# A hybrid decoder step on one core: one tile of a depthwise convolution moved to diagonal matrix products

## The chip, the cores and the metric

The kernel runs on one core of one Trainium2 chip. The metric is the device time of one execution in microseconds. Engines are named as in the profile: PE is the matrix engine (TensorE) and PEld its weight loads, DVE the vector engine, ACT the scalar engine, POOL is GpSimd, and SP issues most transfers. All arithmetic here is float32.

## The reference, cut to what matters

A single layer handles 512 prompt tokens and 8 sample tokens. A projection feeds two groups of channels.

```
z = x @ w_in
# group A: 512 channels
u = z[:, :512] * sigmoid(z[:, 512:1024])
c = causal_depthwise_conv(u, conv_w, width=31) + conv_b   # per channel: sum over k of w[k] * u[t - 30 + k]
c = silu(layer_norm(c))
# group B: 8 heads of 64, state S[value, key], for each token t
S_t = S_{t-1} diag(w_t) + (S_{t-1} a_t) b_t^T + v_t k_t^T ;  y_t = S_t r_t
o = (group_norm(y) + bonus) * gate
x = LN(ALPHA * x + concat(c, o) @ w_out)
x = LN(ALPHA * x + MoE(x))          # 64 experts, top 8, one shared expert
```

## The kernel before, in words

There are three stages. `prepare` projects, shifts and scales, solves small triangular systems and starts the convolution. `recur_and_mix` runs the recurrence, then the output projection, the norm, the router and the shared expert. `experts` streams the 64 experts' weights and multiplies.

**The convolution.** The channels lie on partitions in CT = 4 tiles of 128. `m.u_pad[:, i, :]` holds tile i with 30 zeros ahead of its 512 tokens. One tap (line 176) is one DVE instruction over 128x512: `conv[i] = u_pad[i, k:k+512] * w[:, k] + conv[i]`. There are 4 x 31 = 124 of them, and `Taps.take(n)` issues the next n in order. 74 are taken in `prepare`, fitted between its other DVE work, and 50 in the recurrence: 14 and 5 ahead of step 0, three in each of steps 0 to 9, one in step 10. The sum must be complete in step 10, as step 11 folds it for the norm's mean (line 1930), PE sums over partitions (`conv_sums`), step 13 subtracts it (line 2057), and ACT squares it in step 14.

**The recurrence.** 512 tokens are 16 steps (NCH) of L = 32 tokens. Four steps make a block j of 128 tokens (TM = 4 blocks). Here n is the step, j = n // 4 and c = n % 4. PE, ACT and DVE each run their own list in a fixed order written out by hand, with semaphores between them.

- PE, once a block: `push(j)` (line 1406, 64 products, one per head and chunk) writes `p_push`; ACT copies it to `pushed`; `solve(j)` (line 1415, 64 products with an output of 32x128) writes `p_solved`; ACT copies that to `w1` and `w2` (lines 1710, 1713).
- PE, twice a block: `moves_of(g)` (lines 1431, 1439, 1443) forms the transition and additive parts of two steps and of the reads. ACT copies them (lines 1720, 1721), and DVE adds a part into `r_dec` (`add_reads(g)`, line 1973). `moves_of(g)` waits for the copies and reads of g-1.
- PE, each step: `step(n)` (line 1455) multiplies the state by the step's transition, once the state of n is ready. DVE has meanwhile scaled the old state and added the step's part (lines 2025, 2027), does whatever else is listed for the step (taps, sample tokens' work, group norms), and last adds PE's product (line 2062), which releases `step(n + 1)`.
- PE, once a block: `outputs(j)` (lines 1469, 1475, 1478) reads the four states of the block, in step 4j+4. Its products per tile of two heads are 16 + 16 + 16.
- PE also has, among these, `late_column` (line 1583, the last two projected columns), `turn_tails` and `turn_out` (lines 1486, 1490, 1510), and `gates` (lines 1500, 1501).

In PE's list, step n is: `step(n)`; at n = 12 `conv_sums`; at n = 1 and 3 a late column; at c = 0 `outputs(j-1)` and then `push(j+1)`; at n = 0, 2, 4, 6, 8 a `turn_tails`; at c = 1 `solve(j+1)`; at n = 11 and 15 `gates`; at c = 2 and 3 a `moves_of`; at n = 14 `turn_out`. `outputs(3)` follows step 15, and then `conv_sums` and the output projection `mix_part` (line 1560, 128x512 products with 128x128 weights).

**Space.** The PSUM tensor `ph` has two halves of 1024 columns. `p_push` is the first 512 columns of the second half, `p_solved` all 1024 of it. `w_out` is loaded by SP (line 1284) into the space of the column weights `w_col`, after the last late column and the last solve.

Of the kernel before, what the change touches and what calls it, by code (L numbers as in the profile page):

```python
# [19 lines left out]
ALU = mybir.AluOpType  # L20
# [3 lines left out]
P = 128  # L24
D = 1024
KD = D // P
T = 512
# [4 lines left out]
DC = 512  # L32
# [972 lines left out]
def recur_and_mix(nc, m, ctx_out):  # L1005
# [14 lines left out]
    TAPS_OVER = 10  # L1020
    CONV = 11
    BIG = 1e30
    GONE = -3e38
    QD = D // 4
    with ExitStack() as ctx:
# [107 lines left out]
        sample_y_loaded = early_sem("sample_y_loaded")  # L1133
        tails_stored = [sem(f"tails_stored{b}") for b in range(2)]
        push_done = early_sem("push_done")
        push_taken = early_sem("push_taken")
# [113 lines left out]
        with nc.Block() as block:  # L1250
            @block.sync
            def _(sp):
# [106 lines left out]
            @block.gpsimd  # L1359
            def _(pool):  # L1360
                for spent in m.spent:
                    pool.sem_clear(spent)
                pool.sem_inc(spent_cleared)
                ch = Chain(pool, m.pool_step, m.pool_count)
                pool.wait_ge(w2_done, TM)
# [24 lines left out]

            @block.tensor
            def _(pe):
# [5 lines left out]
                def push(j):  # L1398

                    if j >= 1:  # L1400
                        pe.wait_ge(w1_taken, j)
                        pe.wait_ge(w2_taken, j)
                    for h in range(H):
# [4 lines left out]

                def solve(j):

                    pe.wait_ge(push_taken, j + 1)
                    for h in range(H):
                        for c in range(CM):
                            q, hc = slice(L * c, L * (c + 1)), slice(h * N, (h + 1) * N)
                            last = nc.tensor.matmul(p_solved[q, h, :, :], m.inverse[q, H * j + h, :], two(m.a_rows[q, j, hc], pushed[q, hc]),  # L1415
                                                    start=True, stop=True)
                    last.then_inc(w2_done, 1)

                def moves_of(g):
# [3 lines left out]
                    if g % 2 == 0:  # L1423
                        pe.wait_ge(w1_taken, j + 1)
                        pe.wait_ge(w2_taken, j + 1)
                    if g >= 1:
# [30 lines left out]

                def outputs(j):

# [3 lines left out]
                    if j >= 1:  # L1463
                        pe.wait_ge(centred, ORDER.index(j - 1) + 1)
                    for i in range(CT):
                        for h in (2 * i, 2 * i + 1):
# [4 lines left out]
                        for h in (2 * i, 2 * i + 1):  # L1471
# [7 lines left out]
                    last.then_inc(y_done, 1)  # L1479

# [105 lines left out]

                push(0)
                late_column(0)
                solve(0)
                late_column(1)  # L1590
                moves_of(0)
                moves_of(1)
                for n in range(NCH):
                    j, c = n // CM, n % CM
                    step(n)
                    if n == CONV + 1:
                        pe.wait_ge(conv_folded, 1)
                        pe.wait_ge(w1_taken, TM)
                        pe.wait_ge(w2_taken, TM)
# [12 lines left out]
                    if n in NORMALISE:  # L1612
# [5 lines left out]
                    if n in TURN:  # L1618
                        turn_out(ORDER[TURN[n]])
                outputs(TM - 1)  # L1620
                pe.wait_ge(conv_folded, 2)
# [74 lines left out]
            def _(act):  # L1696
# [3 lines left out]
                def copy_push(j):  # L1700
                    act.wait_ge(push_done, j + 1)
                    if j >= 1:
                        act.wait_ge(w2_done, j)
                    nc.scalar.copy(pushed[:], p_push).then_inc(push_taken, 1)

                def copy_solved(j):
                    act.wait_ge(w2_done, j + 1)
                    if j >= 1:
                        act.wait_ge(move_done, 2 * j)
                    nc.scalar.copy(w1.rearrange("p (h n) -> p h n", h=H), p_solved[:, :, 0, :]).then_inc(w1_taken, 1)  # L1710
                    if j >= 2:
                        act.wait_ge(y_done, j - 1)
                    nc.scalar.copy(w2[:, j % 2, :].rearrange("p (h n) -> p h n", h=H), p_solved[:, :, 1, :]).then_inc(w2_taken, 1)

# [63 lines left out]
                def take_column(u):  # L1778
# [4 lines left out]
                    if b == 1:  # L1783
# [3 lines left out]
                                         scale=m.keep[0:w, s:s + 1]).then_inc(row_taken, 1)  # L1787

                copy_push(0)
                take_column(0)  # L1790
                copy_solved(0)
                take_column(1)
                copy_moves(0)
                copy_moves(1)
                for n in range(NCH):
                    j, c = n // CM, n % CM
                    if n in ROOT:
                        root(ROOT[n])
# [13 lines left out]
                    if c == 1 and j + 1 < TM:  # L1812
                        copy_solved(j + 1)
                    if n in NORMALISE:
# [92 lines left out]
            def _(dve):  # L1907
# [106 lines left out]
                nc.vector.memset(stat[:], 0.0).then_inc(state_ready, 1)  # L2014
                taps.take(14)
                add_reads(0)
                taps.take(5)
                add_reads(1)
                for n in range(NCH):
# [7 lines left out]
                    ch.link(tt(new, new, moves[:, (n // 2) % SETS, n % 2, 1].rearrange("p (i n) -> p i n", i=CT), ALU.add))  # L2027
                    if c == 3 and j + 1 < TM:
                        add_reads(2 * j + 2)
                    if c == 0 and j >= 1:  # L2030
                        add_reads(2 * j + 1)
                    if n in INVERT:
# [15 lines left out]
                    if n == TAPS_OVER:  # L2048
                        taps.take(CT * CW - m.taps_done)
                        ch.link(tt(m.conv[:, :, T:TT], m.u_pad[:, :, CW - 1 + T:CW - 1 + TT], m.params[:, :, CW - 1:CW].broadcast_to([P, CT, B]), ALU.mult))  # L2050
# [8 lines left out]
                    if n in SUM:  # L2059
                        squares(SUM[n])  # L2060
                    dve.wait_ge(step_done, n + 1)
                    tt(new, new, pst[:], ALU.add).then_inc(state_ready, 1)
# [925 lines left out]
```

## Time and profile before

| what | us |
|---|---|
| median of 3 runs (lowest, highest) | 1083.47 (1079.4, 1086.22) |
| the profiled execution, its own time | 1083.88 |
| its span, first to last instruction | 1081.8 |
| PE busy in the span | 1026.4 |
| DVE busy | 710.3 |
| ACT busy | 228.2 |
| POOL busy | 327.6 |

A busy PE is not a PE at its peak: its products are pipelined, and its clock is granted at one of two levels, 2.4 GHz (1.00 in the profile) or 1.2 GHz (0.50). The share of an engine over the whole span says little here, since the stages have different limits. In the trace the recurrence's first product starts at 216.7 us, step 0 of DVE at 235.8, step 15 ends at 321.5, and the output projection starts at 329.8. All starts below are in us from the start of the span.

### The profile page before, as it was taken

The page shows a single profiled execution, that of the slowest core. Times are in us where ns is not written, and L with a number is a line of the kernel's source. Part 1 is how long each engine was busy: PE and PEld are TensorE (multiplying, and loading weights), DVE is VectorE, ACT ScalarE, POOL GpSimd, SP SyncE. Part 2 cuts the span into 40 slices and gives each one's busy share as a digit, 9 for nine tenths or more (in the row PEclk, how much of TensorE's full clock was granted, in tenths as well). Part 3 has the DMA queues.
Part 4 walks back from the last instruction along what each step waited for, and adds up shares of the span by engine and source line. Part 5 has one row for each costly group of instructions (what it writes and reads, how often), then busy time and mean ns, then how long its engine had stood idle before and what let it go on. Part 6 is the DMA issues. An engine that isn't in the chain of part 4 may idle for free.

```text
span 1081.8 us, 31303 instructions
## 1 busy us (share of the span) xinstructions
PE 1026.4 (95%) x13698; PEld 741.5 (69%) x13699; DVE 710.3 (66%) x1547; ACT 228.2 (21%) x480; POOL 327.6 (30%) x330
## 2 busy tenths in 40 slices
PE   8999999878889999999999999999999999999976
PEld 6877888665754458687767777777777777777742
DVE  0789869888876696975578555556555655565326
ACT  2145612122446312101111111011111111111114
POOL 2000010000000001445555455554455555555411
PEclk9999999878859999999999999999999999999997
DMA  7221222250066429599999999999999999999962
GB/s 227 78 60 39 59 60 84 43 163 3 7 205 241 171 83 373 194 356 382 389 390 389 378 384 390 385 386 387 388 385 395 392 387 387 389 389 376 353 197 107
DMA packets 92038, 282.64 MB, mean 261 GB/s; under 512 B 22552, under 2 KB 49689, under 8 KB 67061
## 3 DMA queue, kind: packets, MB, share of 16 engines
q1 hardware_dynamic: 74685, 243.55, 58.1%
q0 software_dynamic: 16272, 33.84, 12.2%
q10 hardware_dynamic: 944, 3.24, 0.8%
q8 instruction: 108, 1.77, 0.6%
q14 instruction: 29, 0.24, 0.1%
HBM read 260.93 MB, written 36.25 MB: 275 GB/s over the span
## 4 chain that ended last, share of the span: by engine, by line
PE 68%; DVE 8%; ACT 2%; DMA 1%; issue 1%; POOLq 0%; DVEq 0%; SPq 0%; ACTq 0%
PE ph L2378 32%; PE ph L2406 21%; PE ph L1542 3%; PE ph L1560 2%; DVE w_exp L176 1%; PE pz_late L1583 1%; PE ph L1683 1%; DMA scr_f<-arena,row 1%; PE pt L1475 1%; PE pz_late L1500 1%; PE pt L2539 1%; PE pz_late L1501 0%; PE pst L1455 0%; PE pt L1478 0%; PE pt L933 0%
## 5 line engine op out<-in xcount | busy, mean ns | idle before, releaser
L2378 PEld LDWEIGHTS ph<-arena,w_exp 128*64 128x64 f32 x8192 | 342.0, 139 | 51.3 <-issue 47.5
L2378 PE MATMUL ph<-arena,w_exp 128*64 128x96 f32 x8192 | 353.9, 248 | 2.1 <-DVE arena L2363 2.1
L2406 PE MATMUL ph<-w_exp,arena 128*96 128x512 f32 x512 | 235.1, 602 | 1.2 <-DVE arena L2396 1.2
L977 POOL DMA_INDIRECT x_area<-scr_x,piece_row x192 | 203.0, 1057 | 82.9 <-issue 54.7
L2433 POOL DMA_INDIRECT scr_f<-arena,row x63 | 93.9, 1490 | 215.1 <-PE ph L2378 166.7
L523 PE MATMUL pz<-w_exp 128*128 128x260 f32 x672 | 155.7, 389 | 0.3 <-ACT w_exp L335 0.3
L2406 PEld LDWEIGHTS ph<-w_exp,arena 128*96 128x96 f32 x512 | 78.4, 163 | 110.2 <-issue 102.1
L523 PEld LDWEIGHTS pz<-w_exp 128*128 128x128 f32 x672 | 128.0, 193 | 22.4 <-issue 2.7
L2424 DVE TENSOR_SCALAR arena<-ph,row_weight 96x512 f32<-96x512 f32 x64 | 47.8, 747 | 138.6 <-PE ph L2406 138.6
L2363 DVE STREAM_TRANSPOSE arena<-x_area 128x768 f32<-128x768 f32 x64 | 104.2, 1628 | 5.3 <-DMA x_area<-scr_x,piece_row 4.6
L2387 ACT ACTIVATE arena<-ph 128x192 f32<-128x192 f32 x64 | 21.1, 330 | 409.6 <-PE ph L2378 402.6
L176 DVE SCALAR_TENSOR_TENSOR w_exp<-arena,w_exp 128x512 f32<-128x512 f32 x120 | 90.0, 750 | 3.6
L2394 DVE TENSOR_TENSOR arena<-arena,ph 128x192 f32<-128x192 f32 x64 | 22.5, 351 | 89.5 <-ACT arena L2387 89.5
L2416 ACT ACTIVATE arena<-ph,row_weight 96x512 f32<-96x512 f32 x64 | 43.6, 682 | 111.6 <-PE ph L2406 101.1
L1560 PE MATMUL ph<-w_exp 128*128 128x512 f32 x128 | 56.9, 596 | 0.0
L955 DVE TENSOR_SCALAR piece_row<-found 32x3 uint32<-32x3 f32 x240 | 40.8, 170 | 4.4
L1560 PEld LDWEIGHTS ph<-w_exp 128*128 128x128 f32 x128 | 23.7, 190 | 28.8 <-issue 28.4
L809 POOL COPY w_exp<-w_exp 128x8 f32<-128x8 f32 x4 | 2.6, 653 | 125.3 <-DVE w_exp L727 125.3
L964 DVE COPY row_weight<-found 32x2 f32<-32x2 f32 x180 | 37.0, 205 | 3.1
L922 DVE TENSOR_TENSOR arena<-slot_index,position 128x480 bf16<-128x480 f32 x60 | 38.4, 645 | 0.0
L1374 POOL MEMSET arena<- 128x64 f32 x1 | 0.2, 151 | 110.0 <-PE ph L1572 110.0
L1366 POOL MEMSET arena<- 128x128 f32 x1 | 0.2, 204 | 106.6 <-PE ph L1415 106.6
(394 smaller groups left out, 1025.4 us busy)
## 6 DMA issues: line engine op xcount, KB each, us to landing
w_exp<-in_exp_up_dram SPq DMA_DIRECT2D x64, 1024.0 KB, 23.9
w_exp<-in_exp_down_dram SPq DMA_DIRECT2D x64, 1024.0 KB, 24.4
w_exp<-in_exp_gate_dram SPq DMA_DIRECT2D x64, 1024.0 KB, 21.8
w_exp<-in_w_in_dram SPq DMA_DIRECT2D x22, 512.0 KB, 3.7
w_exp<-in_x_prompt_dram SPq DMA_DIRECT2D x8, 512.0 KB, 5.4
w_exp<-in_w_out_dram SPq DMA_DIRECT2D x2, 2048.0 KB, 11.6
w_exp<-scr_f SPq DMA_DIRECT2D x8, 512.0 KB, 5.8
x_area<-scr_x,piece_row POOLq DMA_INDIRECT x192, 7.6
```

The source lines that it names most:

```text
L176: self.ch.link(self.nc.vector.scalar_tensor_tensor(out, u, w, out, ALU.mult, ALU.add))
L523: last = nc.tensor.matmul(banks(pz[0:w, c % 2, :])[:, b, :], m.w_col[:, c % WB, k, 0:w], halves(m.x_t[:, k, :])[:, b, :], start=(k == 0), ...
L922: nc.vector.tensor_tensor(m.members[:, e], m.slot_index[:].unsqueeze(1).broadcast_to([P, NT, CAP]), src.unsqueeze(2).broadcast_to([P, NT, ...
L955: last = nc.vector.tensor_scalar(m.piece_row[32 * quad:32 * (quad + 1), s, :], m.found[rows, :, 0], float(QUADS), float(QUADS * TT + quad) ...
L977: nc.gpsimd.indirect_dma_start(m.x_pieces[:, s, r, :], None, m.scr_x1.rearrange("t (q c) -> (t q) c", q=QUADS), bass.IndirectOffsetOnAxis( ...
L1560: last = nc.tensor.matmul(ph[0:n, i % 2, c * 512:(c + 1) * 512], lhs, w_out[c][:, kw, :], start=(part == 0 and k == 0), stop=(part == 1 an ...
L2363: nc.vector.transpose(x_list_t[:, s % 2].rearrange("p k (r t) -> p r k t", r=RUNS), m.x_pieces[:, s].rearrange("p r (c k) -> p r k c", k=K ...
L2378: last = nc.tensor.matmul(pgu[64 * half:64 * half + 64, s % 2, (2 * part + j) * CAP:(2 * part + j + 1) * CAP], w[job.slot][:, k, f0:P * ha ...
L2406: last = nc.tensor.matmul(pyl[0:CAP, c, :], hid[:, s % 2, j, :], m.expert_down[job.slot][:, j, c * 512:(c + 1) * 512], start=(j == 0), sto ...
L2416: nc.scalar.activation(y_list[:, s % 2, 0:512], pyl[0:CAP, 0, :], ACT.Copy, scale=row_weight[0:CAP, job.l, 1:2]).then_inc(y_act, 1)
L2424: nc.vector.tensor_scalar(y_list[:, s % 2, 512:1024], pyl[0:CAP, 1, :], row_weight[0:CAP, job.l, 1:2], None, ALU.mult).then_inc(y_dve, 1)
L2433: nc.gpsimd.indirect_dma_start(m.scr_f[s % 2], bass.IndirectOffsetOnAxis(ap=row[:, job.l:job.l + 1], axis=0), y_list[:, s % 2, :], None, b ...
```

## The change

Tile 3 of the convolution leaves the `Taps` list. For tap k ACT builds a diagonal 128x128 matrix, the identity scaled per partition by w[:, k], into one of 8 buffers, and PE multiplies it with `u_pad[:, 3, k:k+512]`, all 31 products accumulating in `p_conv`, a PSUM bank. In step 10 DVE copies that bank to `conv[3]` with the bias added. Of the 31 products, 2 stand behind `push(0)`, 4 between `moves_of(0)` and `moves_of(1)`, and 3, 2, 3, 2, 3, 3, 3, 3, 3 in steps 0 to 8. DVE keeps 93 taps: 74 in `prepare` as before, 9 ahead of step 0, and one in each of steps 0 to 9.

`p_solved` shrinks to 512 columns, and so `solve(j)` runs in two halves of four heads, each copied by ACT before the next overwrites it. `outputs(j)` is also in two halves, of tiles 0 and 1 in step 4j+4 and of tiles 2 and 3 in step 4j+5, with `push` ahead of the first. `add_reads` moves from the head to the end of its step's DVE list. The loads of `w_out` wait for the last diagonal too, since the diagonals lie in that space.

```diff
+    DIAGS = 8
+    LAST_TILE = CT - 1
+    CONV_TAPS = {0: 3, 1: 2, 2: 3, 3: 2, 4: 3, 5: 3, 6: 3, 7: 3, 8: 3}
...
-        p_solved = ph[:, 1, :].rearrange("p (h w n) -> p h w n", h=H, w=2)
+        p_solved = ph[:, 1, 0:DC].rearrange("p (h w n) -> p h w n", h=H // 2, w=2)
+        p_conv = ph[:, 1, DC:2 * DC]
+        diag = place(m, m.AT_COL, DIAGS, P)
...
-                sp.wait_ge(w2_done, TM)
+                sp.wait_ge(w2_done, 2 * TM)
+                sp.wait_ge(diag_used, CW)
...
+                def solve(j, half):
+                    if half == 0:
+                        pe.wait_ge(push_taken, j + 1)
+                    else:
+                        pe.wait_ge(w1_taken, 2 * j + 1)
+                        pe.wait_ge(w2_taken, 2 * j + 1)
...
+                def conv_taps(count):
+                    for _ in range(count):
+                        k = taps_used[0]
+                        pe.wait_ge(diag_ready, k + 1)
+                        nc.tensor.matmul(p_conv, diag[:, k % DIAGS, :], m.u_pad[:, LAST_TILE, k:k + T], start=(k == 0), stop=(k == CW - 1)).then_inc(diag_used, 1)
+                        taps_used[0] += 1
...
                 push(0)
+                conv_taps(2)
+                solve(0, 0)
                 late_column(0)
-                solve(0)
+                solve(0, 1)
                 late_column(1)
                 moves_of(0)
+                conv_taps(CW - 2 - sum(CONV_TAPS.values()))
                 moves_of(1)
...
                     if c == 0:
-                        if j >= 1:
-                            outputs(j - 1)
                         if j + 1 < TM:
                             push(j + 1)
+                        if j >= 1:
+                            outputs(j - 1, 0)
+                    if c != 1:
+                        conv_taps(CONV_TAPS.get(n, 0))
...
-                    if c == 1 and j + 1 < TM:
-                        solve(j + 1)
+                    if c == 1:
+                        if j + 1 < TM:
+                            solve(j + 1, 0)
+                        if j >= 1:
+                            outputs(j - 1, 1)
+                        conv_taps(CONV_TAPS.get(n, 0))
+                        if j + 1 < TM:
+                            solve(j + 1, 1)
...
+                def make_diags(upto):
+                    while diags_made[0] < min(upto, CW):
+                        k = diags_made[0]
+                        if k >= DIAGS:
+                            act.wait_ge(diag_used, k - DIAGS + 1)
+                        nc.scalar.activation(diag[:, k % DIAGS, :], m.ident[:], ACT.Copy, scale=m.params[:, LAST_TILE, k:k + 1]).then_inc(diag_ready, 1)
+                        diags_made[0] += 1
...
-                taps.take(14)
+                taps.take(9)
                 add_reads(0)
-                taps.take(5)
                 add_reads(1)
...
-                        taps.take(min(3, CT * CW - m.taps_done))
+                        taps.take(min(1, LAST_TILE * CW - m.taps_done))
...
+                        dve.wait_ge(diag_used, CW)
+                        ch.link(nc.vector.tensor_scalar(m.conv[:, LAST_TILE, 0:T], p_conv, m.params[:, LAST_TILE, par("conv_b"):par("conv_b") + 1], None, ALU.add))
```

## Rows read from the trace of the kernel before

**Rows 1.** Stages by windows: us; busy PE, PEld, DVE, ACT, POOL (instructions); PEclk, DMA share, GB/s.
```profile
235.80:292.70 56.90, 45.92 (x1295) 34.11 (x1288) 50.86 (x86) 14.43 (x29) 0.00 (x0) 0.79 0.02 5
406.00:1081.80 675.80, 655.98 (x9320) 468.47 (x9319) 402.33 (x1054) 87.44 (x176) 308.23 (x263) 0.99 0.95 357
```

**Rows 2.** Timeline of DVE: start us, us, engine line operation, count [idle before <-releaser].
```profile
217.24 10.89 DVE L176 SCALAR_TENSOR_TENSOR w_exp<-arena,w_exp 128x512 f32<-128x512 f32 x14
...
235.77 0.42 DVE L2025 TENSOR_TENSOR x_area<-x_area 128x256 f32<-128x256 f32 x1
...
315.21 0.42 DVE L2062 TENSOR_TENSOR x_area<-x_area,pst 128x256 f32<-128x256 f32 x1 [2.95 <-PE pst L1455]
```

**Rows 3.** Timeline of PE, prologue and steps 1 to 6.
```profile
217.77 3.77 PE L1583 MATMUL pz_late<-w_exp 128*128 128x260 f32 x16
...
230.69 0.89 PE L1431 MATMUL ph<-w_exp,arena 32*64 32x96 f32 x32 [1.81 <-DVE w_exp L1973]
...
241.92 1.12 PE L1455 MATMUL pst<-x_area,w_exp 64*64 64x64 f32 x16 [3.83 <-DVE x_area L2062]
...
264.44 0.35 PE L1469 MATMUL pt<-x_area,w_exp 64*32 64x64 f32 x16 [0.67 <-ACT w_exp L1721]
...
265.30 0.34 PE L1469 MATMUL pt<-x_area,w_exp 64*32 64x64 f32 x16
...
268.44 0.34 PE L1469 MATMUL pt<-x_area,w_exp 64*32 64x64 f32 x14 [1.14 <-issue]
...
269.18 1.07 PE L1406 MATMUL ph<-w_exp 32*32 32x64 f32 x64
270.18 0.60 PE L1490 MATMUL pz_late<-ident,w_exp 128*9 128x128 f32 x4
...
272.19 1.95 PE L1415 MATMUL ph<-w_exp,arena 32*32 32x128 f32 x64
274.06 0.68 PE L1455 MATMUL pst<-x_area,w_exp 64*64 64x64 f32 x16
...
275.37 0.89 PE L1431 MATMUL ph<-w_exp,arena 32*64 32x96 f32 x32
...
276.87 0.33 PE L1443 MATMUL pt<-w_exp 32*64 32x64 f32 x8
```

**Rows 4.** Timeline of PE, the gates of step 11, and the first products of the output projection.
```profile
298.22 2.07 PE L1500 MATMUL pz_late<-arena,w_exp 128*128 128x512 f32 x2
...
329.84 3.59 PE L1560 MATMUL ph<-w_exp 128*128 128x512 f32 x8
```

**Rows 5.** Timeline of the weight loads beside those products.
```profile
330.27 0.19 PEld L1560 LDWEIGHTS ph<-w_exp 128*128 128x128 f32 x1 [0.24 <-issue]
```

**Rows 6.** Timeline of ACT, eight small scaled copies.
```profile
295.06 2.02 ACT L1761 ACTIVATE w_exp<-w_exp,arena 128x64 f32<-128x64 f32 x8
```

**Rows 7.** Timeline of PE, the starts of step 11 and of steps 13 to 15, `outputs(2)` at 307.51.
```profile
297.25 1.04 PE L1455 MATMUL pst<-x_area,w_exp 64*64 64x64 f32 x16 [0.15 <-DVE x_area L2062]
...
307.51 0.47 PE L1469 MATMUL pt<-x_area,w_exp 64*32 64x64 f32 x16
...
314.04 1.12 PE L1455 MATMUL pst<-x_area,w_exp 64*64 64x64 f32 x16
315.77 1.12 PE L1455 MATMUL pst<-x_area,w_exp 64*64 64x64 f32 x16 [0.61 <-DVE x_area L2062]
...
318.74 1.12 PE L1455 MATMUL pst<-x_area,w_exp 64*64 64x64 f32 x16 [0.81 <-DVE x_area L2062]
```

**Rows 8.** Windows at one level of the granted clock each, columns as in rows 1.
```profile
246.00:249.00 3.00, 3.00 (x42) 1.79 (x44) 2.83 (x6) 0.73 (x2) 0.00 (x0) 0.97 0.00 0
...
262.80:277.00 14.20, 11.70 (x498) 9.66 (x488) 11.97 (x24) 3.80 (x7) 0.00 (x0) 1.00 0.03 7
...
280.30:290.60 10.30, 9.98 (x335) 8.51 (x330) 9.20 (x17) 1.07 (x2) 0.00 (x0) 0.50 0.02 5
...
304.20:328.00 23.80, 21.20 (x403) 13.83 (x404) 18.49 (x34) 10.13 (x33) 0.00 (x0) 0.50 0.42 138
```

More of the change, by code:

```diff
@@ L1134, in recur_and_mix @@
         tails_stored = [sem(f"tails_stored{b}") for b in range(2)]
+        diag_ready = early_sem("diag_ready")
+        diag_used = sem("diag_used")
         push_done = early_sem("push_done")
@@ L1400, in push @@
                     if j >= 1:
-                        pe.wait_ge(w1_taken, j)
-                        pe.wait_ge(w2_taken, j)
+                        pe.wait_ge(w1_taken, 2 * j)
+                        pe.wait_ge(w2_taken, 2 * j)
                     for h in range(H):
@@ L1407, in push @@
                     last.then_inc(push_done, 1)
-                def solve(j):
-                    pe.wait_ge(push_taken, j + 1)
-                    for h in range(H):
+                def solve(j, half):
[4 more added lines that the diff above has]
+                        pe.wait_ge(w2_taken, 2 * j + 1)
+                    for h in range(H // 2):
                         for c in range(CM):
-                            q, hc = slice(L * c, L * (c + 1)), slice(h * N, (h + 1) * N)
-                            last = nc.tensor.matmul(p_solved[q, h, :, :], m.inverse[q, H * j + h, :], two(m.a_rows[q, j, hc], pushed[q, hc]),
+                            q, at = slice(L * c, L * (c + 1)), H // 2 * half + h
+                            hc = slice(at * N, (at + 1) * N)
+                            last = nc.tensor.matmul(p_solved[q, h, :, :], m.inverse[q, H * j + at, :], two(m.a_rows[q, j, hc], pushed[q, hc]),
                                                     start=True, stop=True)
                     last.then_inc(w2_done, 1)
+                taps_used = [0]
+                def conv_taps(count):
[4 more added lines that the diff above has]
+                        taps_used[0] += 1
                 def moves_of(g):
@@ L1423, in moves_of @@
                     if g % 2 == 0:
-                        pe.wait_ge(w1_taken, j + 1)
-                        pe.wait_ge(w2_taken, j + 1)
+                        pe.wait_ge(w1_taken, 2 * j + 2)
+                        pe.wait_ge(w2_taken, 2 * j + 2)
                     if g >= 1:
@@ L1456, in step, with outputs @@
                     last.then_inc(step_done, 1)
-                def outputs(j):
+                def outputs(j, half):
                     pe.wait_ge(state_ready, CM * j + CM)
@@ L1464, in outputs @@
                         pe.wait_ge(centred, ORDER.index(j - 1) + 1)
-                    for i in range(CT):
+                    for i in (2 * half, 2 * half + 1):
                         for h in (2 * i, 2 * i + 1):
@@ L1478, in outputs @@
                                 last = nc.tensor.matmul(p_out[q, h % 2, i, :], m.by_head[q, j, h, READS_B], w2[q, j % 2, hc], start=False, stop=True)
-                    last.then_inc(y_done, 1)
+                    if half == 1:
+                        last.then_inc(y_done, 1)
                 def turn_tails(t):
@@ L1619, in _ @@
                         turn_out(ORDER[TURN[n]])
-                outputs(TM - 1)
+                for half in range(2):
+                    outputs(TM - 1, half)
                 pe.wait_ge(conv_folded, 2)
@@ L1702, in copy_push, with copy_solved @@
                     if j >= 1:
-                        act.wait_ge(w2_done, j)
+                        act.wait_ge(w2_done, 2 * j)
                     nc.scalar.copy(pushed[:], p_push).then_inc(push_taken, 1)
-                def copy_solved(j):
-                    act.wait_ge(w2_done, j + 1)
+                def copy_solved(j, half):
+                    hs = slice(H // 2 * half, H // 2 * (half + 1))
+                    act.wait_ge(w2_done, 2 * j + half + 1)
                     if j >= 1:
                         act.wait_ge(move_done, 2 * j)
-                    nc.scalar.copy(w1.rearrange("p (h n) -> p h n", h=H), p_solved[:, :, 0, :]).then_inc(w1_taken, 1)
+                    nc.scalar.copy(w1.rearrange("p (h n) -> p h n", h=H)[:, hs, :], p_solved[:, :, 0, :]).then_inc(w1_taken, 1)
                     if j >= 2:
                         act.wait_ge(y_done, j - 1)
-                    nc.scalar.copy(w2[:, j % 2, :].rearrange("p (h n) -> p h n", h=H), p_solved[:, :, 1, :]).then_inc(w2_taken, 1)
+                    nc.scalar.copy(w2[:, j % 2, :].rearrange("p (h n) -> p h n", h=H)[:, hs, :], p_solved[:, :, 1, :]).then_inc(w2_taken, 1)
+                diags_made = [0]
+                def make_diags(upto):
[5 more added lines that the diff above has]
+                        diags_made[0] += 1
                 def copy_moves(g):
@@ L1787, in take_column @@
                                          scale=m.keep[0:w, s:s + 1]).then_inc(row_taken, 1)
+                make_diags(2)
                 copy_push(0)
+                make_diags(DIAGS)
+                copy_solved(0, 0)
                 take_column(0)
-                copy_solved(0)
+                copy_solved(0, 1)
                 take_column(1)
@@ L1794, in _ @@
                 copy_moves(1)
+                issued = CW - sum(CONV_TAPS.values())
                 for n in range(NCH):
                     j, c = n // CM, n % CM
+                    make_diags(issued + DIAGS)
+                    issued += CONV_TAPS.get(n, 0)
                     if n in ROOT:
@@ L1812, in _ @@
                     if c == 1 and j + 1 < TM:
-                        copy_solved(j + 1)
+                        for half in range(2):
+                            copy_solved(j + 1, half)
                     if n in NORMALISE:
@@ L2027, in _ @@
                     ch.link(tt(new, new, moves[:, (n // 2) % SETS, n % 2, 1].rearrange("p (i n) -> p i n", i=CT), ALU.add))
[L2028 to L2031, printed above, removed]
                     if n in INVERT:
@@ L2048, in _ @@
                     if n == TAPS_OVER:
-                        taps.take(CT * CW - m.taps_done)
+                        taps.take(LAST_TILE * CW - m.taps_done)
+                        dve.wait_ge(diag_used, CW)
+                        ch.link(nc.vector.tensor_scalar(m.conv[:, LAST_TILE, 0:T], p_conv, m.params[:, LAST_TILE, par("conv_b"):par("conv_b") + 1], None, ALU.add))
                         ch.link(tt(m.conv[:, :, T:TT], m.u_pad[:, :, CW - 1 + T:CW - 1 + TT], m.params[:, :, CW - 1:CW].broadcast_to([P, CT, B]), ALU.mult))
@@ L2060, in _ @@
                         squares(SUM[n])
+                    if c == 3 and j + 1 < TM:
+                        add_reads(2 * j + 2)
+                    if c == 0 and j >= 1:
+                        add_reads(2 * j + 1)
                     dve.wait_ge(step_done, n + 1)
```

6 lines of the change are left out of this document (3 added, 3 removed).

## The prediction

> **What bounds the kernel now.** I read the views in this order: the stages, DVE's timeline in the recurrence, PE's timeline beside it, and last the granted clock. The time from 406 us on is the experts' stage, with PE busy 656 of 675.8 us and the transfers at 0.95 [rows 1]. Its transfers are released by work behind the recurrence, so whatever the recurrence gains or loses moves that stage as a whole, one for one. The stage that the change touches is steps 0 to 9 (235.8 to 292.7) and its neighbours. There DVE is busy 50.9 of 56.9 us and PE 45.9, at a mean clock of 0.79 [rows 1]. Two engines near their limit take turns: PE waits 3.83 us for DVE ahead of step 1 [rows 3], and DVE waits 2.95 us for PE in step 13 [rows 2]. The reader should see that DVE is the bound in the first ten steps, but with PE only 5 us of busy time behind it. After step 11 it is PE, at half clock for 23.8 us [rows 8].
>
> **What DVE is relieved of.** A tap is 0.78 us at DVE's pace (14 in 10.89) [rows 2]. Of 50 in the recurrence 31 go: 10 ahead of step 0, 20 in steps 0 to 9, one in step 10. In steps 0 to 9 that is 20 x 0.78 = 15.6 us. DVE's busy time there falls from 50.9 to about 35.3. In step 10 a copy of the bank with the bias, about the price of a tap, takes the place of the last tap: nothing.
>
> **What PE is charged.** The nearest row to a tap on PE is a product of the same shape, 128x128 weights against 128x512: eight in 3.59 us, whose last ends late, so 0.43 us each; at half clock the gates' products of that width take 2.07 for two, 1.0 each [rows 4]. The weight load of 0.19 us starts 0.24 us after the one before has ended, so it hides under the running product [rows 5]. I take 0.43 at full clock and 1.0 at half. The Trainium skill has two rules that speak against this. "FP8 and Floating Point Precision", TensorE Precision Notes, has true FP32 as four passes through the array, which by an estimate from its clock would be about 0.85 us a tap and would make the sum 10 us worse; the trace disagrees, with 0.43. "TensorE: Matmul & The Clock Gate", The mechanism, lets a weight load overlap a running product only if they use different rows of the array; that would add the load's 0.19 us to each tap, and rows 5 disagree with that too.
>
> Between two kinds of product I add 0.15 us per group of taps, for the first weights, which have nothing of their own kind to hide under. That is an estimate; its ends are 0 and 0.3, about one load and a half.
>
> **PE's work in steps 1 to 9, at full clock.** Nine steps at 0.65 = 5.9 (0.68 is the time of one group, [rows 3]). Two pushes at 1.0 (269.18 to 270.18) = 2.0. Three solves at 1.87 (272.19 to 274.06) = 5.6. Two late columns at 3.7 = 7.4. Two `outputs` at 3.44 (0.86 from one tile to the next, times four) = 6.9. Four `moves_of` at 1.83 (275.37 to 277.20) = 7.3. Four turns of tails at about 0.6 = 2.3. All are in rows 3. 22 taps at 0.43 = 9.5, and eight groups at 0.15 = 1.2. That is 48.1. PE also stops for "issue", 1.14 us once in this stretch [rows 3], so far under DVE's cover; on the bound it counts, with something for a second one: 1.4. The second half of `solve(3)` waits for ACT's copies with no tap to cover it: 0.5. Sum 50.0 us, against DVE's 35 in ten steps. **PE becomes the bound.**
>
> Step 0 is still DVE's. PE's step 1 started at 241.92; with two taps less on DVE it starts at 240.4. Adding 50.0 gives 290.4 for the start of step 10. It holds `step` and `moves_of(6)`, 0.65 + 1.83, and DVE's list there (one group norm's centring, whose input is ready when PE starts the step, then the bank's copy) ends about as early. Step 11 starts at 292.9 instead of 297.25 [rows 7]: **4.3 us gained**.
>
> **The split outputs.** `outputs(2)` held PE from 307.51 to 314.04, 6.5 us at half clock, with step 13 behind it, and DVE idle 2.95 us [rows 7, 2]. In halves, step 13 starts 3.3 us earlier and DVE's wait goes. What is late next is step 14 on PE: 307.51 + 6.53 + 1.12 = 315.2 instead of 315.77, and DVE's centring in step 14, which needs the second half. Step 15 then starts at about 317.4 instead of 318.74, 1.3 us earlier at half clock; with a full clock DVE is the bound and the whole 2.95 us comes back. I take 1.8.
>
> **The prologue.** Four of the taps stand ahead of `moves_of(1)`, where PE waited 1.81 us for DVE [rows 3]; 4 x 0.43 + 0.15 = 1.87 fills just that. Two stand behind `push(0)`, ahead of a late column and uncovered: 0.86 + 0.15. The prologue gets longer by 1.1 us. DVE's 10 taps less there gain nothing, as DVE waited at its end for PE's and ACT's work. If the filled gap keeps the clock up, up to 1.5 us comes back, and I do not count on it.
>
> **Costs with cover.** ACT builds 31 diagonals. Eight scaled copies over 64 columns take 2.02 us [rows 6], 0.25 each; for 128 columns between 0.25 and 0.5, taken 0.3, so 9 us over the recurrence. ACT is busy 14.4 of 56.9 us in steps 0 to 9 [rows 1]; a diagonal is built up to eight ahead, and the wait on its buffer is for taps of the step before, which stand ahead of the products that ACT would copy next, so nothing queues behind it. If that cover failed, each diagonal would cost PE 0.3. Halved solves double ACT's copies, under the outputs and taps between the halves. `add_reads` at the end of the step is late by one tap and a centring at most, and `moves_of` comes after the step's taps on PE: nothing. SP's and POOL's new waits are met by the last solve in step 9, after the last tap in step 8: nothing.
>
> **The clock.** The sum so far is 4.3 + 1.8 - 1.1 = 5.0 us at full clock, and the clock decides what stays. At half, 22 taps cost 12.5 us more, two `outputs` 5, nine steps 4, and the other 22 us of products between nothing and 22 more, taken 11: 50 us becomes about 83. If a share f of the time is at half, the stretch takes 50 / (1 - 0.4 f). Before, the clock of 0.79 means f = 0.42. Dense products lift it: `step(1)` at 241.92 took 1.12 us, the price at half, where one at full takes 0.68 [rows 3]; a late column followed it, and from 246 the clock is 0.97 [rows 8]. Small products with short gaps held it full from 262.8 to 277, but others kept PE busy 9.98 of 10.3 us at half [rows 8]. With wide taps in eight of nine steps and PE never idle for long I take f = 0.1, 2 us. **Net gain 3 us.** The profiled execution took 1083.88 us, 2.1 beside its span and 0.4 above the median. 1083.88 - 3.0 - 0.4 = 1080.5, rounded to 1080.
>
> **Rivals.**
> 1. The clock stays as it is now, f = 0.42: the stretch takes 60 us and the result is 5 - 10 = 5 us worse, 1088. For it: the same small products still make up 39 of 48 us of PE's work. Against: PE's gaps are filled. Chance 0.22, with all f from 0.23, where the gain is gone, to 0.6.
> 2. PE sinks to half clock in most of steps 1 to 9, as it did for 23.8 us while 89% busy [rows 8], and each tap costs 1.0 us instead of 0.43. It decides at f = 0.6, where 50 us are 66 and the result passes 1094.5; at f = 1 it is 1083.5 - 5 + 33 = 1111. Against it is what one late column did at 246. Chance 0.09.
> 3. The full clock holds through steps 11 to 15 and the outputs behind them, too. 23.8 us at half would shrink by a factor of 0.6 to 0.7, some 7 us on the path, and the 2 us above are not lost: 1083.5 - 5 - 7 = 1071.5. For it: fewer stops in front of PE. Against: there are no taps after step 8, and the clock fell there in spite of dense gates. Chance 0.15.
> 4. DVE stays the bound, as it would if the taps on PE hid in its idle time: then 15.6 + 1.8 - 1.1 = 16 us are gained, 1067. PE's 50 us of work speak plainly against it. Chance 0.03, and within the chance of faster.
>
> My forecast has 0.51. A measurement of this kernel can tell about 1%, 10.8 us, from no change. Faster by more than that, under 1072.6: rivals 3 and 4, 0.16, as rival 3 lies right at the bound. Slower by more, above 1094.3: 0.09. Within: 0.75. The range runs from 1070, leaving out rival 4 and the better half of rival 3, to 1090, leaving out rival 2 and the worse part of rival 1.
>
> **What the profile after would show.** Step 0 of DVE at 236 to 237; step 10 of PE near 291; PE waiting for DVE before no step from 2 to 9, and DVE idle for PE's steps instead; L176 with 93 executions; a clock above 0.9 from 240 to 290; wide taps 0.43 us apart; no wait of 2.95 us in step 13; everything from the output projection on shifted alike. The forecast is wrong if the clock in steps 1 to 9 is below 0.88, if a tap takes more than 0.5 us at full clock, if ACT's diagonals come late, or if the experts' stage changes its own length.

## The result: 0.4% slower

The changed kernel takes 1086.87 us, the median of 18 runs (1081.95 to 1091.08), the kernel before 1082.9 (18 runs, 1078.19 to 1086.22). The ratio is 1.0037, interval 1.0023 to 1.0051: 4 us slower, where 3 us of gain were forecast. The time lies in the range, the direction was wrong. The profiled execution took 1086.67 us.

The page of the changed kernel (busy us and instructions; granted clock in 40 slices of 27 us):

```profile
span 1084.9 us, 31445 instructions
...
PE 1038.9 (96%) x13760; PEld 741.2 (68%) x13761; DVE 690.2 (64%) x1517; ACT 238.0 (22%) x519; POOL 328.1 (30%) x330
...
PEclk9998999899989999999999999999999999999997
```

DVE lost 20 us of work, PE gained 12.5, and PE has **62** instructions more (13760 against 13698) though the change gave it 31 products. That is the error of the prediction in one number. (PE's busy time rose by less than the price of its new work, while the mean clock from `push(0)` to the output projection rose from 0.76 to 0.96.) The prologue, steps 0 to 9 and the experts' stage by windows, columns as in [rows 1]:

```profile
218.81:239.88 21.07, 21.06 (x431) 15.28 (x431) 7.75 (x14) 8.39 (x24) 0.00 (x0) 1.00 0.64 204
239.88:300.57 60.69, 57.84 (x1210) 35.71 (x1214) 36.23 (x66) 21.48 (x55) 0.00 (x0) 1.00 0.02 5
...
412.00:1084.90 672.90, 653.04 (x9309) 465.36 (x9308) 403.41 (x1054) 86.27 (x173) 308.76 (x263) 0.99 0.95 358
```

Against [rows 1] DVE fell as forecast (36.2 us busy, forecast 35.3), the clock is at its full level throughout (forecast: a tenth of the time at half), and still the ten steps take 60.69 us where they took 56.9. PE is busy 57.84 of them. What fills it, by groups of PE instructions in the same window (count | busy, mean ns of one):

```profile
L1439 PE MATMUL ph<-arena,w_exp 128*128 128x512 f32 x50 | 23.9, 611 | 0.0
L1607 PE MATMUL pz_late<-w_exp 128*32 128x260 f32 x32 | 7.4, 384 | 0.0
L1478 PE MATMUL pst<-x_area,w_exp 64*64 64x64 f32 x144 | 6.1, 224 | 0.9 <-DVE x_area L2118 0.9
```

The list has 25 taps in steps 0 to 8; the trace has 50 instructions for them, and 32 for the 16 products of the two late columns. **Each float32 product is two instructions in the trace**, and 0.43 us is the pace of one instruction, not of one product. PE's timeline says the same, in the three taps of step 0 and of step 8, and shows where steps 10 and 11 start:

```profile
240.46 2.84 PE L1439 MATMUL ph<-arena,w_exp 128*128 128x512 f32 x6
...
296.21 2.84 PE L1439 MATMUL ph<-arena,w_exp 128*128 128x512 f32 x6
...
304.30 0.68 PE L1478 MATMUL pst<-x_area,w_exp 64*64 64x64 f32 x16
...
306.92 0.68 PE L1478 MATMUL pst<-x_area,w_exp 64*64 64x64 f32 x16
```

Three taps hold PE for 2.7 us (240.46 to 243.14, where the next product starts), 0.89 each with the change to another kind of product in it. The weight loads beside them show the pace of one instruction, 0.19 us of load and 0.24 between two loads, 0.43 (PEld's timeline):

```profile
241.43 0.19 PEld L1439 LDWEIGHTS ph<-arena,w_exp 128*128 128x128 f32 x1 [0.24 <-issue]
```

DVE, which before the change waited for PE's step 1.3 us in step 9 and nowhere else in these ten, now waits for it in steps 5, 6 and 9, 10.8 us in all. It waits about as long (10.6 us in steps 3, 4, 7 and 8, where it was 2.3 before) for ACT's copies of what PE's `moves_of` made, ahead of `add_reads`; ACT itself waits for PE there. The longest of the second kind and the two longest of the first (columns as in [rows 2]):

```profile
267.53 0.42 DVE L2028 TENSOR_TENSOR w_exp<-w_exp,ph 128x256 f32<-128x256 f32 x1 [4.15 <-ACT w_exp L1769]
...
274.51 0.42 DVE L2118 TENSOR_TENSOR x_area<-x_area,pst 128x256 f32<-128x256 f32 x1 [3.80 <-PE pst L1478]
...
300.12 0.42 DVE L2118 TENSOR_TENSOR x_area<-x_area,pst 128x256 f32<-128x256 f32 x1 [4.90 <-PE pst L1478]
```

Where the time of the two profiled executions went, from DVE's and PE's starts in the two traces:

| stretch | before | changed | difference |
|---|---|---|---|
| start of the span to `push(0)` (the same code) | 216.75 | 218.81 | +2.1 |
| `push(0)` to DVE's step 0 | 19.02 | 21.07 | +2.1 |
| steps 0 to 9 | 56.96 | 60.69 | +3.7 |
| step 10 | 4.41 | 5.49 | +1.1 |
| steps 11 to 15 | 23.92 | 21.77 | -2.2 |
| then to the output projection | 8.78 | 6.79 | -2.0 |
| the rest | 751.96 | 750.28 | -1.7 |

From `push(0)` to the output projection the change costs 2.7 us: 115.81 against 113.09. The first and last lines are outside it. In the traces of this study `push(0)` starts anywhere from 216.75 to 222.2 us after the same code, so a whole time of one execution can't settle such a change, and the stretch from `push(0)` to the projection is what I compare below. It has its own limit: each stretch is that of one traced execution, and the two of the changed kernel, 115.8 and 114.8, differ by 1.0 us, so differences of that size say nothing.

### The profile page after: what moved, and what is told of

Its sections match the earlier page's. It is cut to its first block, busy times and chain, and to the rows that moved or that the text cites. A ratio compares the mean times of both kernels' runs of the same rounds, so it can differ in the third digit from the quotient of the medians.

```text
span 1084.9 us, 31445 instructions
## 1 busy us (share of the span) xinstructions
PE 1038.9 (96%) x13760; PEld 741.2 (68%) x13761; DVE 690.2 (64%) x1517; ACT 238.0 (22%) x519; POOL 328.1 (30%) x330
## 4 chain that ended last, share of the span: by engine, by line
PE 71%; DVE 5%; ACT 2%; DMA 1%; issue 1%; POOLq 0%; DVEq 0%; SPq 0%
PE ph L2434 31%; PE ph L2462 21%; PE ph L1566 3%; PE ph L1439 2%; PE ph L1584 2%; PE pz_late L1607 1%; PE ph L1719 1%; PE pst L1478 1%; PE ph L1428 1%; PE pt L1498 1%; PE ph L1454 1%; DMA scr_f<-arena,row 1%; DMA w_exp<-scr_f 1%; PE pt L2595 1%; PE pt L1492 0%
## 5 line engine op out<-in xcount | busy, mean ns | idle before, releaser
L2443 ACT ACTIVATE arena<-ph 128x192 f32<-128x192 f32 x64 | 21.1, 330 | 408.7 <-PE ph L2434 401.9
L176 DVE SCALAR_TENSOR_TENSOR w_exp<-arena,w_exp 128x512 f32<-128x512 f32 x90 | 67.4, 749 | 2.8
L1584 PE MATMUL ph<-w_exp 128*128 128x512 f32 x128 | 56.9, 596 | 0.0
L1584 PEld LDWEIGHTS ph<-w_exp 128*128 128x128 f32 x128 | 23.7, 190 | 28.8 <-issue 28.4
## 6 DMA issues: line engine op xcount, KB each, us to landing
w_exp<-in_exp_up_dram SPq DMA_DIRECT2D x64, 1024.0 KB, 26.3
w_exp<-in_w_out_dram SPq DMA_DIRECT2D x2, 2048.0 KB, 11.6
```

What stands on the lines that cost most here:

```text
L176: self.ch.link(self.nc.vector.scalar_tensor_tensor(out, u, w, out, ALU.mult, ALU.add))
L1584: last = nc.tensor.matmul(ph[0:n, i % 2, c * 512:(c + 1) * 512], lhs, w_out[c][:, kw, :], start=(part == 0 and k == 0), stop=(part == 1 an ...
```

## The experiments

**Theory A**: a tap on PE is 0.86 us, and those in steps 1 to 9 lie on its path; halves and copies are harmless. **Rival R**: the loss is in the halved solves and outputs, their doubled copies and the later `add_reads`. **Rival R2**: what a tap costs is weights, diagonals or the switch of product, not passes through the array.

Stretches in us, with the clock in steps 0 to 9, and the ratio of the whole time to the kernel before, run beside it:

| kernel | taps on PE | `push(0)` to step 0 | steps 0 to 9 (clock) | `push(0)` to projection | ratio, interval |
|---|---|---|---|---|---|
| before | 0 | 19.0 | 57.0 (0.79) | 113.1 | |
| changed | 31 | 21.1 | 60.7 (1.00) | 115.8 | 1.0037, 1.0023 to 1.0051 |
| changed, again | 31 | 21.1 | 60.5 (1.00) | 114.8 | 1.0027, 1.0007 to 1.0046 |
| halves only | 0 | 22.3 | 55.9 (0.82) | 112.3 | 1.0024, 1.0002 to 1.0046 |
| one tap | 1 | 19.7 | 47.0 (0.90) | 107.8 | 1.0395, 1.0362 to 1.0428 (see text) |
| each tap twice | 62 | 26.2 | 80.3 (1.00) | 144.6 | 1.0282, 1.0246 to 1.0318 |
| eight on PE | 8 | 19.7 | 51.8 (0.97) | 109.2 | 0.9978, 0.9952 to 1.0004 |
| sixteen on PE | 16 | 19.9 | 54.3 (0.97) | 109.8 | 0.9926, 0.9901 to 0.9950 |
| eight, tuned | 8 | 18.8 | 52.8 (0.97) | 106.2 | 0.9913, 0.9889 to 0.9937 |
| bfloat16 taps | 31 | 18.8 | 49.9 (0.93) | 103.2 | 0.9884, 0.9858 to 0.9909 |
| bfloat16, tuned | 31 | 18.9 | 45.9 (1.00) | 103.1 | 0.9899, 0.9853 to 0.9945 |

Several chips ran them; in two of the sets of runs the kernel before takes 1149 and 1154 us, as the experts' stage is longer there (from the projection on, the kernels traced in those sets take 813 us or more, the others 749 to 752). Only ratios and stretches are compared across.

**Halves only.** The changed kernel without taps on PE:

```diff
-                conv_taps(...)          # all four places, and make_diags
-                taps.take(9)
+                taps.take(14)
                 add_reads(0)
+                taps.take(5)
...
-                        taps.take(min(1, LAST_TILE * CW - m.taps_done))
+                        taps.take(min(3, CT * CW - m.taps_done))
```

> The changed kernel without any tap on TensorE: DVE has its 50 taps in the recurrence again, and solves and outputs are in halves as in the changed kernel. Theory A (each tap on PE is a product of two instructions, 0.86 us, and 22 of them lie on PE's path in steps 1 to 9; the halves are harmless): steps 0 to 9 take 57 to 58 us as before, DVE-bound, the wait of step 13 goes, and the time is 1 to 3 us below the kernel before (1080 to 1082). Rival R (the loss comes from the halved solves with their doubled copies, and from the later add_reads): 2 to 4 us above the kernel before (1085 to 1087), with steps 0 to 9 above 59 us.

Measured: steps 0 to 9 in 55.9 us, 1 less than before, so rival R fails there, and the 3.7 us that the changed kernel loses in them are not from the halves. The whole is another matter. It is 0.24% slower, 2.8 us, which is what R expected (2 to 4) and not A (1 to 3 faster), while the stretch of the traced execution is 0.8 us shorter than before. That execution was one of the faster ones (1146.34 us, median 1152.48), and what makes the median slower was not found. The interval (0.02% to 0.46%) also covers the changed kernel's 0.37%, so how much of its 4 us comes with the halves stays open. One cost of them can be seen, in the prologue (windows of the prologue and of steps 0 to 9, columns as in [rows 1]; then PE's timeline in the prologue):

```profile
218.33:240.64 22.31, 19.80 (x392) 16.49 (x396) 15.19 (x24) 5.60 (x14) 0.00 (x0) 0.76 0.59 193
240.64:296.56 55.92, 43.78 (x1199) 32.49 (x1195) 50.97 (x86) 15.26 (x33) 0.00 (x0) 0.82 0.02 5
```

```profile
220.12 1.93 PE L1427 MATMUL ph<-w_exp,arena 32*32 32x128 f32 x32 [0.69 <-ACT w_exp L1734]
221.98 5.90 PE L1606 MATMUL pz_late<-w_exp 128*128 128x260 f32 x16
```

With `solve(0)` moved ahead of the late column, PE waits for the copy that the late column used to hide, and in this execution the clock is at half, so that column takes 5.90 us where it took 3.77 [rows 3]. The prologue is 3.3 us longer, and what is gained behind step 10 makes up for it in this execution. In the changed kernel two taps stand in that place, which hid it.

**One tap, and each tap twice.**

```diff
# one tap
-                conv_taps(2)            # and all others; one tap is left, in step 5
...
# each tap twice
+                        nc.tensor.matmul(p_conv, diag[:, k % DIAGS, :], m.u_pad[:, LAST_TILE, k:k + T], start=(k == 0), stop=False)
-                        nc.tensor.matmul(... start=(k == 0), stop=(k == CW - 1)).then_inc(diag_used, 1)
+                        nc.tensor.matmul(... start=False, stop=(k == CW - 1)).then_inc(diag_used, 1)
```

> The changed kernel with 30 of the 31 taps on PE left out (tile 3 of the convolution is not computed); DVE keeps its 93 taps. Theory A: PE's work in steps 1 to 9 falls from 59.7 to 41 or 42 us, DVE's is about 36, so steps 0 to 9 take 43 to 46 us instead of 60.7, and the time is 14 to 17 us below the changed kernel, 1070 to 1073, or up to 1078 if the granted clock falls as in the kernel before. With a tap at the 0.43 us of the prediction only 9 to 10 us would go, 1077. Rival R: less than 5 us go, above 1082.

> The changed kernel with each of the 31 products issued twice into the same bank (tile 3 of the convolution comes out doubled). Theory A: 31 x 0.86 = 26.7 us more, nearly all on PE's path, so 24 to 27 us above the changed kernel, 1111 to 1114. With a tap at 0.43 us: 12 to 13 us, 1099 to 1100. If PE were not the bound in these steps (rival R): under 8 us.

With one tap the convolution comes out otherwise and so does the experts' stage: 867 us follow the start of the projection, with 9690 instructions on PE, where the halves-only kernel on the same chip has 814 and 9605. So its whole time, 4% above the kernel before, is left aside. With each tap twice it is 813 us and 9605 instructions, and the whole time counts. The ten steps by windows, columns as in [rows 1], first with one tap, then with each tap twice:

```profile
241.83:288.84 47.01, 40.60 (x1187) 29.69 (x1181) 36.26 (x66) 15.26 (x33) 0.00 (x0) 0.90 0.03 6
```

```profile
246.88:327.16 80.28, 79.46 (x1272) 45.29 (x1276) 36.25 (x67) 21.50 (x55) 0.00 (x0) 1.00 0.01 4
```

Doubling 25 products in steps 0 to 8 costs 80.28 - 60.69 = 19.6 us, 0.78 each, and raises PE's busy time by 79.46 - 57.84 = 21.6, **0.86 each**; the other 2 us fill its idle time. In the prologue it costs 26.2 - 21.1 = 5.2 for six, 0.86 each; 0.43 would have made 10.8 and 2.6. The stretch is 28.8 us longer, more than the 24 to 27 expected: 4.0 of it lie behind step 10, at a lower clock (0.60 behind step 15, instead of 1.00). The whole time is 2.8% above the kernel before, where the changed kernel is 0.4% above, so it says about the same, 28 us. With 24 taps fewer the steps lose 13.7 us, not 24 x 0.86 = 20.6, since in 47 us PE's 40.6 and DVE's 36.3 us alternate and the clock is no longer full; the forecast of 43 to 46 was a little low for that. The stretch loses 8 us only, as steps 11 to 15 take 26.3 us (21.8 with 31 taps) and what follows 9.2 at a clock of 0.52 (6.8 at 1.00). In these steps A holds and R fails.

**Fewer taps on PE, in float32.** Here PE takes the last 8 or 16 of tile 3's taps and DVE the others, and DVE adds the bank instead of copying it.

```diff
+    CONV_TAPS = {0: 1, 2: 1, 6: 1, 7: 2, 8: 1}      # eight; sixteen: {0: 3, 2: 3, 4: 1, 6: 2, 7: 3, 8: 2}
+    DVE_TAPS = [2, 3, 2, 2, 3, 3, 2, 2, 2, 3]       # sixteen: [1, 2, 1, 2, 2, 2, 1, 1, 2, 2]
...
-                taps.take(9)
+                taps.take(14)
                 add_reads(0)
+                taps.take(4)
```

> Eight of tile 3's taps on PE (two between moves_of(0) and moves_of(1), none ahead of them, and one or two in steps 0, 2, 6, 7, 8, where PE's list is short), 42 on DVE in the recurrence (18 ahead of step 0, 24 in steps 0 to 9). Theory A: PE in steps 1 to 9 is 40.6 + 6 x 0.86 = 46 us, DVE 30 + 24 x 0.78 = 49 us, so steps 0 to 9 take 49 to 52 us instead of 57 before, and the time is 5 to 9 us below the kernel before, 1074 to 1078. If it is the wide products that keep the clock up, it falls again here and 3 us of that are lost: 1077 to 1081. Rival R: no better than the kernel before.

> Sixteen of tile 3's taps on PE (two between moves_of(0) and moves_of(1), fourteen in steps 0, 2, 4, 6, 7, 8), 34 on DVE in the recurrence (18 ahead of step 0, 16 in steps 0 to 9). Theory A (0.86 us a tap on PE's path): PE in steps 1 to 9 is 40.6 + 11 x 0.86 = 50 us, DVE 30 + 16 x 0.78 = 42.5, so PE is the bound, steps 0 to 9 take 53 to 55 us (eight on PE: 51.75; thirty-one: 60.7), and the time is 2 us below to 2 us above the kernel before. With a tap at 0.43 us it would be better than eight on PE, at 49 to 50 us for the ten steps.

Steps 0 to 9 take 51.8 and 54.3 us, both as expected for 0.86. The whole times did not come out as expected. Eight on PE gained 3.9 us in the stretch, but 2.5 in the whole (0.9978), not 5 to 9, and its ratio does not exclude no change. Sixteen is 8 us below (0.9926), better than its expectation of at most 2. In the traced stretches the two are level, 109.2 and 109.8: eight's ten steps are shorter, but its step 10 takes 6.7 us (sixteen's 5.4) and its steps 11 to 15 take 24.8 at a clock of 0.64 (23.9 at 0.81). They ran on two chips, and why the whole times favour sixteen stays open.

**Eight, tuned.** The same, with the prologue's cover put back:

```diff
+    CONV_TAPS = {0: 1, 2: 1, 6: 1, 7: 1, 8: 1}
...
                 push(0)
+                late_column(0)
                 solve(0, 0)
-                late_column(0)
+                conv_taps(1)
                 solve(0, 1)
...
-                taps.take(14)
+                taps.take(17)
```

> Eight of tile 3's taps on PE, placed for cover: one between the halves of solve(0), where PE would wait for ACT's copies, two between moves_of(0) and moves_of(1), five in steps 0, 1, 2, 6... as in the kernel with eight but one less in step 7; late_column(0) back behind push(0); DVE has 21 taps ahead of step 0 and 21 in steps 0 to 9. Theory A: the prologue takes 19 to 20 us, steps 0 to 9 take 48 to 51, and the time is 5 to 9 us below the kernel before, a version that beats both. If the granted clock falls in the steps, or the halves cost what they gain, it is level with the kernel with eight on PE, 2 to 3 us below the kernel before.

0.9913 (0.9889 to 0.9937), 9.4 us below the kernel before, just beyond the 5 to 9 expected, and faster than the kernel before and the changed one. Sixteen, on the same chip and without this tuning, has an interval that overlaps, so which of the two float32 versions is the best can't be told. Its prologue is 18.8 us at full clock. The ten steps take 52.8, above the 48 to 51 expected (windows of the prologue and of steps 0 to 9):

```profile
219.48:238.26 18.78, 18.72 (x431) 14.37 (x431) 16.54 (x26) 7.83 (x22) 0.00 (x0) 1.00 0.72 228
238.26:291.03 52.77, 41.92 (x1164) 29.42 (x1168) 44.32 (x78) 15.26 (x33) 0.00 (x0) 0.97 0.02 6
```

PE is busy 41.9 and DVE 44.3 of 52.8 us. Neither is full; they wait for each other in turn, which a sum of one engine's work misses by 8 us.

**bfloat16 taps.** The taps of tile 3 are rounded: ACT writes diagonals and one copy of u in bfloat16.

```diff
-        diag = place(m, m.AT_COL, DIAGS, P)
+        diag = m.w_exp[:, m.AT_COL:m.AT_COL + DIAGS * P // 2].bitcast(BF16).rearrange("p (k c) -> p k c", k=DIAGS)
+        u_half = m.w_exp[:, m.AT_COL + DIAGS * P // 2:m.AT_COL + DIAGS * P // 2 + (CW - 1 + T) // 2].bitcast(BF16)
```

> The changed kernel with the same 31 products, but their operands in bfloat16: ACT rounds tile 3 of u once (one copy of 128x542 ahead of the diagonals) and writes the diagonals as bfloat16, so taps of tile 3 are rounded. Theory A: a float32 product is two instructions of 0.43 us in the trace because it takes more passes, and a bfloat16 one is a single instruction of about 0.22 us; PE in steps 1 to 9 falls from 59.7 to 40.6 + 22 x 0.22 = 45 to 46 us, and steps 0 to 9 take 48 to 50 us, so the stretch from push(0) to the output projection is 10 to 13 us shorter than in the changed kernel. If what the taps cost lay in weight loads, waits for diagonals or the switches between kinds of product (rival R2), it would be less than 6 us shorter.

The stretch is 103.2 us, 11.6 less than the changed kernel on the same chip. The taps in the trace, one instruction each now (groups of instructions from 215 to 320 us, columns as above for groups, then step 0's three taps in PE's timeline):

```profile
L1443 PE MATMUL ph<-w_exp 128*128 128x512 bf16 x31 | 8.6, 382 | 0.0
...
L1443 PEld LDWEIGHTS ph<-w_exp 128*128 128x128 bf16 x31 | 2.2, 97 | 2.6 <-issue 0.6
```

```profile
241.64 0.82 PE L1443 MATMUL ph<-w_exp 128*128 128x512 bf16 x3
```

Three in 0.82 us, of which the last is 0.38: 0.22 from one to the next, a quarter of the float32 tap. Diagonals, groups and switches are the same in number, so they are not what a tap costs. The weight loads did change, two of 0.19 us for each float32 tap and one of 0.10 here, so this run alone does not exclude them. The late column does: it has float32 weights of the same 128x128 shape, and 260 columns, and goes at 0.23 us an instruction (16 in 3.77, [rows 3]), against 0.43 at 512 columns. The pace goes nearly with the columns, while the loads stay as they are. R2 fails.

**bfloat16, tuned.** The prologue as above, and DVE's ten taps in the steps moved ahead of step 0. One of PE's taps in step 4 and one in step 8 move into the prologue as well, where eight stand now.

```diff
-                taps.take(9)
+                taps.take(15)
                 add_reads(0)
+                taps.take(4)
                 add_reads(1)
...
-                    if n < TAPS_OVER:
-                        taps.take(min(1, LAST_TILE * CW - m.taps_done))
```

> The kernel with bfloat16 taps, its prologue as in the tuned kernel: late_column(0) right behind push(0), four taps between the halves of solve(0), four between moves_of(0) and moves_of(1), 23 in steps 0 to 8; DVE takes its 19 remaining taps ahead of step 0, where it waited 13 us in the changed kernel, and none in the steps. Theory A (PE is the bound, so PE's shorter list tells and DVE's does not): the prologue is 19 us, steps 0 to 9 take 47 to 50 (bfloat16 taps before: 49.9), and the time is 11 to 15 us below the kernel before. If DVE's ten taps in the steps had been on the path (rival R3), steps 0 to 9 would fall by 5 to 8 us, to 42 to 45, and the time would be 18 us or more below.

The ten steps are 45.9 us, between the two expectations (47 to 50, and 42 to 45), so neither holds. Of the 4.0 us less than with bfloat16 taps before, DVE's ten taps, PE's two and the fuller clock (1.00, it was 0.93) can each have a part, and they are not separated. The stretch is 103.1 us, no shorter than without the tuning, as the 9.9 us after step 15 ran at a clock of 0.50 where that run's 4.8 had the full clock. Which of the two is the better can't be told; the ratios overlap.

**The changed kernel again.**

> The changed kernel as it is, on the chip of these runs, where the experts' stage runs at another pace: all theories expect 3 to 5 us above the kernel before, and 115 to 116 us from push(0) to the output projection.

1.0027, 2.9 us above, and 114.8 us in the stretch, both just under what was expected. The interval overlaps the first (1.0037): the changed kernel is slower on both occasions.

## Why the prediction was wrong, step by step

- **"What PE is charged", 0.43 us a tap: the step that failed.** "Eight in 3.59 us" [rows 4] were read as eight products; they are four, and eight instructions. The count was there to see: `push` has 8 heads x 4 chunks = 32 products in the code and x64 in [rows 3], a late column 8 and x16. The description ahead of the prediction says 64 products for `push` and `solve` and 16 + 16 + 16 for a tile of `outputs`; it is 32 each, and 8 + 8 + 8. (A transpose is one instruction: `turn_tails(0)` has four in the code and four in the trace.) The price at half clock has the same fault: the 2.07 us of the gates [rows 4] are one product, not two. The missing term is 22 x 0.43 = 9.5 us in steps 1 to 9, and 2.6 in the prologue. Forecast 50.0 us from step 1 to step 10 on PE; with the term 59.5; measured 244.65 to 304.30, **59.65**. With it the sum forecasts a loss of 7.1 us in the stretch, of which 2.7 came: the ten steps and step 10 lose 4.8 (by the mended sum 5.2), and the prologue and what follows step 15 lost less than it says. That the whole is slower than before, and not only short of the gain, rests on 4 us, and there the halves may have a part.
- **The rule that was rejected.** The Trainium skill ("FP8 and Floating Point Precision", TensorE Precision Notes) has true FP32 as four passes, and the prediction let the trace overrule it. The trace bears it out: a bfloat16 tap 0.22 us, a float32 tap 0.86, four times as long.
- **DVE's relief**: right. 36.2 us busy, forecast 35.3, and 93 taps in the trace (90 and 3 first ones).
- **PE becomes the bound**: it did. Step 1 was forecast at 240.4 and step 10 at 290.4, measured at 244.65 and 304.30: both 4 us late from ahead of step 0, and step 10 another 9.65 by the taps' price. The other terms (solves, outputs, moves, columns, stops for "issue") were priced from groups timed start to start, so the doubled count did them no harm, and they held.
- **The prologue**: forecast +1.1, measured +2.1. Four taps take 3.6 us, not 1.87, in a gap of 1.8, and two take 1.9, not 1.0; that is 3.7 us, and some comes back, as the clock is 1.00 there instead of 0.91.
- **The split outputs**: forecast 1.8 in steps 11 to 15, measured 2.2, with the mean clock at 0.76 instead of 0.58, so not all of it need be the split's. The wait of 2.95 us in step 13 [rows 2] is gone; the one in step 12, for ACT's copy, was 2.71 and is 2.95. The halves-only kernel gains 1.6 there (clock 0.87), and pays 3.3 in its prologue and 1.0 in step 10.
- **Costs with cover**: a diagonal is 0.33 us (six in 1.86), forecast 0.3, and PE waited for them 0.7 us in all. Held. Step 10 is 1.1 us longer, on `outputs(1, 1)` in step 9, for which DVE waits 1.05 us; the forecast had that end "about as early".
- **The clock**: forecast a tenth at half, measured none, from `push(0)` to step 12. Rivals 1 and 2 did not come about, rival 4 was excluded as argued, and of rival 3 a part came true: 2.0 us between step 15 and the projection, at a clock of 1.00 instead of 0.60. Had the taps been priced right, the clock would have been the smaller question.
- **Left open**: the two traced executions differ by 2.8 us, the medians by 4; 2.7 are in the stretch. What the 2.1 us ahead of `push(0)` and the -1.7 behind the projection are was not settled; the former scatters by more than that over executions of the same code.

## What to carry to other kernels

Before a row becomes the price of an operation, hold its count against the number of calls in the code: here float32 products come as two instructions each, and a pace per instruction is half a price. When work moves from one engine to another that is nearly as busy, move the amount that balances them, not the whole: sixteen taps gained 0.7%, and eight with a tuned prologue 0.9%, where thirty-one lost 0.4%. Eight without the tuning did not stand clear of no change. And two engines that hand a recurrence to each other are not full at the bound; with eight taps the steps took 8 us more than the busier one's work.

## What the runs showed of the hardware

A float32 product of 128x512 holds PE for 0.86 us at the full clock, and one in bfloat16 for 0.22. The weight loads (two of 0.19 us, and one of 0.10) hide under the running product of the same kind: with the same loads the pace of an instruction is 0.23 us at 260 columns and 0.43 at 512. With two or three float32 taps in each of steps 0 to 8 the granted clock stayed at 1.00 for 94 us, from `push(0)` at 218.8 to step 12 at 313. In steps 0 to 9 the same small products without them had 0.79 before and 0.82 with the halves alone; with one tap, and PE's list otherwise the same, it was 0.90. PE's idle time differs between these runs as well, so what kept the clock up is not separated.
